# Differential attention: a head's weights are made between the maxima of the next head's two scores

## The chip, the cores and the metric

The kernel runs on one core of a Trainium2 chip. The metric is the device time of one execution in microseconds (us); less is better. Engines are TensorE (PE, its weight loads PEld), VectorE (DVE), ScalarE (ACT), GpSimd (POOL) and SyncE (SP).

## What is computed

Two stacks of two layers each run one after the other over 256 tokens of width 1024. The change lies in the first stack, in its differential attention, which each of its two layers holds once, beside two other kinds of attention and gates. Cut to that branch:

```python
def _diff_branch(q, k, v, lam, subln, lambda_init, cos, sin):
    q = _apply_rope(q.reshape(b, s, DIFF_HEADS, 2, DIFF_D), cos, sin)     # 8 heads, 2 scores each, 64 wide
    k = _apply_rope(k.reshape(b, s, DIFF_HEADS, 2, DIFF_D), cos, sin)
    v = v.reshape(b, s, DIFF_HEADS, 2 * DIFF_D)
    lambda_full = jnp.exp(jnp.sum(lf[0] * lf[1])) - jnp.exp(jnp.sum(lf[2] * lf[3])) + lambda_init
    def attend(qblk):
        sc = jnp.einsum('bqhcd,bkhcd->bhcqk', qblk, k).astype(jnp.float32) * scale
        p = jax.nn.softmax(sc, axis=-1)
        w = (p[:, :, 0] - lambda_full * p[:, :, 1]).astype(v.dtype)
        return jnp.einsum('bhqk,bkhe->bqhe', w, v)
    o = _rms(_sweep_query_blocks(attend, q), subln, 1e-5) * (1.0 - lambda_init)
```

A head has two scores of 256 x 256, two softmaxes, and one matrix of weights, the first softmax less lambda times the second.

## The kernel before

All 256 tokens stay on chip; the projections' weights (about 400 MB) stream in. They come as **panels** of 512 KB (128 x 1024 fp32) through a ring of five buffers `wring`. ACT copies a panel to `whi` (rounded), DVE takes the rest to `wlo` (`split_lo`, 128x1024 TENSOR_TENSOR, L121), and PE multiplies each chunk three times (hi x hi, hi x lo, lo x hi). A panel of a projection is 24 matmuls of 128x256 (L112). ACT's part stands three panels ahead in the order, DVE's two.

`schedule` writes one list of steps. Each engine's program goes through that list and issues its own part of each step, so the list is the order of every engine's queue, and an engine does a later step only when it is through with, or waits no more for, the earlier ones. Two generators are woven: `weave((diff(), 1), (pgate(), 0.75))` takes one turn of the differential attention and then three quarters of a turn of `pgate`, the projections for the gates and one branch product (`xT` and `oM` panels). Each `yield` is such a turn. Of three turns of `pgate` two bring a panel.

Inside `diff`, `staged(8, ...)` runs eight heads through stages. A stage is a function, a lag and a flag:

```python
def staged(n, *stages):
    for i in range(n + max(lag for _, lag, _ in stages)):
        for f, lag, rest in stages:
            if 0 <= i - lag < n:
                f(i - lag)
                if rest or i >= n:
                    yield
```

The stages of head h, with what each issues:

- `scores(0)`, `scores(1)`: PE writes a score of head h to a PSUM bank (L112 `ps<-kT,qT`, four records of 64x256 in the trace for each of the two). DVE takes the row maxima (TENSOR_REDUCE L133, 128x512, and a small TENSOR_SCALAR L124, 128x2): below, a **max**. ACT makes `E` = exp with the sums (two ACTIVATE L118).
- `weights`: `diff_weights` on DVE waits for both exps of the head, then runs two RECIPROCAL (L139), two TENSOR_SCALAR of 128x256 (L124), a small TENSOR_SCALAR with `small`, and two SCALAR_TENSOR_TENSOR of 128x256 (L130).
- `turn_unit`, the **turn**: PE waits for the head's weights and transposes them (four L115 `ps<-cst,E`); DVE copies the result to `PT` (L127, 128x512).
- `values`: PE multiplies `PT` with the values (L112 `ps<-PT,dv`), ACT takes the result to `dsq` (squares) and `draw`.
- `norm`, once in two heads: PE sums the squares, ACT takes the root by Ln and Exp with two table loads. `gain`, once in two heads, on DVE: a product (L130, `draw`), a cast (L127) and a difference (L121) to `oD`.

The score buffers `E` form a ring of four, so two heads are in flight. The branch product's output is taken by DVE to `acc` (L130, 128x512).

Of the kernel before, what the change touches and what calls it, by code (L numbers as in the profile page):

```python
# [330 lines left out]
# [8 lines that stand above are left out]
# [77 lines left out]
def schedule(K, a):  # L416
# [5 lines left out]
    def do(kind, *args):  # L422
        steps.append((kind, args))
# [61 lines left out]
    def turned(src, n, ready, out, w=128):  # L485

        for c in range(0, n, 2):
            m = min(2, n - c)
            u = AB.take()
            do("turn", u, src, c, m, w, ready)  # L490
            out(c, m, u)
            yield
# [16 lines left out]
    def features_to(dst, func=ACT.Copy, scale=1.0, w=128, tag=None):  # L509
        return lambda c, m, u: do("features_out", dst, tag or dst.name, c, m, u, func, scale, w)  # L510
# [11 lines left out]
    def mem_keys(l, x):  # L522
        yield from projB(a["mem_w_kv"][l], 0, 512, x, features_to(memkv[l].mk))

    def mem_values(l, x):
        yield from projA(a["mem_w_kv"][l], 512, 512, x, tokens_to(memkv[l].mv, 512))
# [11 lines left out]
    prow, values = ar.take("prow", 128), mem_values(0, memT)  # L538
# [24 lines left out]
    def rms_open(tag, at, sums, buf=None):  # L563

        n = Box()
        n.tag, n.h = tag, hN.tok()
        n.hold = [buf or ar.take("rms", 2048, at=at), ar.take("rmss", 16, at=sums)]
        n.u3, b = n.hold[0].tok(), n.hold[1].ap
        n.ss, n.pre, n.tmp, n.rs = b[:, 0:4], b[:, 4:6], b[:, 6:8], b[:, 8:10]
        return n  # L570
# [26 lines left out]
    def block1(l, xN, xT, later):  # L597
# [39 lines left out]
        def score_unit(key, q, k, scale, ready):  # L637

            v = Box()
            v.key, v.s = key, ES.take()  # L640
            v.E = v.s.ap[:, 0:512].rearrange("p (t k) -> p t k", t=2)
            v.mx, v.rs = v.s.ap[:, 512:514], v.s.ap[:, 514:516]
            do("scores", v, AB.take(), q, k, scale, ready)
            return v

        def turn_unit(v):

            v.p = PS.take()
            v.PT = v.p.ap.rearrange("p (s q) -> p s q", s=2)
            u = AB.take()  # L650
            do("turn_weights", v, u)
            v.s.freed = u.full
            return v
# [36 lines left out]
        def diff():  # L690
            for k, b in enumerate((dq, dk)):
                do("diff_rope", c, b, kT, k)
                yield
            do("diff_lambda", c, kT)
            c.lam = sm[:, 82:83]
            yield from turned(dq.tok(), 8, lambda h, t: [("diff_rope", l, 0)], features_to(qT, tag=("diff", l, "q")))
            yield from turned(dk.tok(), 8, lambda h, t: [("diff_rope", l, 1)], features_to(kT, tag=("diff", l, "k")))
            ar.give(dq, dk)
            c.oD = None
            un, sqs = {}, {}  # L700
            rings = [[ar.take(k, 512) for _ in range(2)] for k in ("dsq", "draw")]
            SQ, RAW = (Slots(r) for r in rings)

            def scores(i):
                def go(h):
                    un[h, i] = score_unit(("diff", l, h, i), qT.ap[64 * i:64 * i + 64, h * 256:h * 256 + 256],
                                          kT.ap[64 * i:64 * i + 64, h * 256:h * 256 + 256], 0.125, [(("diff", l, x), h) for x in "qk"])
                return go

            def weights(h):  # L710
                do("diff_weights", c, un[h, 0], un[h, 1])
                un[h, 1].s.freed = ("weights", un[h, 0].key, 1)

            def values(h):
                if h % 2 == 0:
                    sqs[h] = (SQ.take(), RAW.take())
                sq, raw = sqs[h // 2 * 2]
                u = AB.take()
                v = un[h, 0]
                do("values", v, dv.tok()[:, :, h * 128:h * 128 + 128], u, lambda: [(dv.name, t, h // 4) for t in range(2)])  # L720
                v.p.freed = u.full
                do("diff_values_out", c, h, u, sq, raw)

            def norm(h):
                if h % 2:
                    do("diff_norm", c, h - 1, AB.take(), sqs[h - 1][0])

            def gain(h):
                if h % 2:
                    sq, raw = sqs[h - 1]  # L730
                    c.oD = c.oD or ar.pair("oD", 8)
                    do("diff_gain", c, h - 1, sq, raw)
                    sq.freed = raw.freed = (c.oD.name, h - 1)
            yield from staged(8, (scores(0), 0, True), (scores(1), 0, True), (lambda h: turn_unit(un[h, 0]), 1, True), (values, 2, True),
                              (norm, 3, False), (weights, 0, False), (gain, 4, False))
            ar.give(qT, kT, dv, *rings[0], *rings[1])

        mqT = ar.take("mqT", 1024)
# [6 lines left out]
        def pgate():  # L745
            yield from projB(w, MQ, 512, xT, features_to(mqT))
            for i in range(2):
                gT.append(gT[0].again() if i else ar.take("gate", 2048, top=True))
                yield from projB(w, GATE + 1024 * i, 1024, xT, lambda k, m, u: do("gate_out", c, i, gT[i], k, m, u))
                if i == 0:  # L750
                    yield from branch(acc, wb, 0, oM, gT[0], 0, keep=True)
                    ar.give(oM)
        weave((diff(), 1), (pgate(), 0.75))
        oD, oE, g2 = c.oD, ar.pair("oE", 4), ar.take("gate", 2048)

# [31 lines left out]
        if l == 0:  # L787
# [5 lines left out]
            keys, values = mem_keys(1, memT), mem_values(1, memT)  # L793
# [76 lines left out]
    norm = rms_open(("mix", 0), None, 34304, n.res.again())  # L870
# [445 lines left out]
    for l in range(DEPTH):  # L1316
        norm = block2(l, norm)
# [1577 lines left out]
```

How the kernel before makes its waits and increments, by code:

```python
    def wait_ge(self, sem, n):  # L106
        if self.e is not None and self.seen.get(id(sem), 0) < n:
            self.e.wait_ge(sem, n)
            self.seen[id(sem)] = n
# [1232 lines left out]
    def bank_free(u):  # L1342
        if u.before:
            e.wait_ge(*at(u.before))
# [1 line left out]
    def tokens(p, x, us, q0, first, fin):  # L1346
        e.wait_ge(*at(("lo", p.i)))
        for t in range(2):
            o = us[t].ap[:, 0:p.nb]
            if first:
                bank_free(us[t])
            for k in range(p.nk):
                e.wait_ge(*at((x.name, q0 + k)))
                xh, xl = x.at(q0 + k, t * 128, 128)
                e.matmul(o, xh, p.hi[:, k, :], start=first and k == 0, stop=False)
                e.matmul(o, xh, p.lo[:, k, :], start=False, stop=False)
                m = e.matmul(o, xl, p.hi[:, k, :], start=False, stop=fin and k == p.nk - 1)
            m.then_inc(*up("pe_panel", ("panel", p.i, t)))
# [1 line left out]
    def features(p, x, u, q0, chunks):  # L1360
        e.wait_ge(*at(("lo", p.i)))
        if q0 == 0:
            bank_free(u)
        for j0 in range(0, p.nb, 128):
            w = min(128, p.nb - j0)
            o = u.ap[0:w, 2 * j0:2 * j0 + 256]
            for k in range(p.nk):
                q = q0 + k
                e.wait_ge(*at((x.name, q)))
                xh, xl = x.at(q)
                ch, cl = p.hi[:, k, j0:j0 + w], p.lo[:, k, j0:j0 + w]
                e.matmul(o, ch, xh, start=q == 0 and j0 == 0, stop=False, skip_group_check=True)
# [292 lines left out]
    def mem_kept():  # L1665
        e.wait_ge(*at("memkept"))
```

## Time and profile before

| | us |
|---|---|
| median of 3 runs | 2539.05 (2537.12 to 2541.59) |
| the profiled execution | 2531.99, span 2530.2 |
| PE busy, share of the span | 2458.0, 97% |
| DVE busy | 1798.4, 71% |
| ACT busy | 1442.6, 57% |
| differential attention's heads, layer 0 | about 174 to 238 us from the span's start |
| the same, layer 1 | about 683 to 747 us |

Starts in the timeline are in us from the span's start. A bracket behind an instruction gives how long its engine stood idle before it, and what released it. Of two consecutive DVE instructions the second's start is the safer mark, since the listed durations overlap a little.

### The profile page before, as it was taken

Reading aid. Unit: us, or ns where it says so; the run is one execution under the profiler, and the core shown is the slowest. Engines: PE = TensorE matmul, PEld = TensorE weight load, DVE = VectorE, ACT = ScalarE, POOL = GpSimd, SP = SyncE. Lnnn points to the kernel's source line nnn. Section 1 sums busy time; section 2 is a strip of 40 time slices with the busy share of each in tenths; the row PEclk is TensorE's granted clock in tenths of the full one; section 3 lists DMA queues with packets and bytes.
Section 4 is the critical chain, followed back from the end, with each engine's and each line's share of the span. In section 5 each row is a group of like instructions: output and inputs, shape, how many; then the busy total and the mean of one; then the engine's idle time right before and its main releaser. Section 6 shows DMA issues by size and latency. Waiting matters only on the chain.

```text
span 2530.2 us, 42246 instructions
## 1 busy us (share of the span) xinstructions
PE 2458.0 (97%) x17296; PEld 2253.4 (89%) x17296; DVE 1798.4 (71%) x2929; ACT 1442.6 (57%) x2106; POOL 268.5 (11%) x222
## 2 busy tenths in 40 slices
PE   8999999999999999899999999999999999999998
PEld 8888989888889898799999798998898999898986
DVE  4567675565676755587778896885697778886874
ACT  5547555445475554466656654664766656545654
POOL 0000002000000000001114710000011207500000
PEclk9999999999999999999999999999999999999999
DMA  7544576655445566554466645666554567545664
GB/s 249 158 129 118 165 241 199 202 181 159 127 119 164 171 196 201 161 152 126 126 196 194 198 131 176 190 205 185 146 151 118 156 190 202 178 152 171 191 201 132
DMA packets 358917, 430.44 MB, mean 170 GB/s; under 512 B 20617, under 2 KB 286311, under 8 KB 358469
## 3 DMA queue, kind: packets, MB, share of 16 engines
q1 hardware_dynamic: 341312, 401.72, 52.3%
q10 hardware_dynamic: 14340, 14.93, 2.4%
q0 software_dynamic: 3072, 11.10, 1.4%
q8 instruction: 137, 2.24, 0.4%
q14 instruction: 56, 0.45, 0.1%
HBM read 424.44 MB, written 3.24 MB: 169 GB/s over the span
## 4 chain that ended last, share of the span: by engine, by line
PE 85%; DVE 8%; ACT 4%; issue 1%; DMA 1%; POOL 0%; POOLq 0%; ACTq 0%; DVEq 0%
PE ps L112 84%; DVE wlo L121 2%; PE ps L115 2%; ACT L118 1%; ACT whi L118 1%; ACT hgKm L118 1%; ACT E L118 0%; ACT lnv L118 0%; DVE hgQB L121 0%; DMA kT<-in_diff_lambda 0%; DVE hgQF L121 0%; DVE E L124 0%; DVE sbc L130 0%; DVE E L133 0%; DVE gate L130 0%
## 5 line engine op out<-in xcount | busy, mean ns | idle before, releaser
L121 DVE TENSOR_TENSOR wlo<-wring,whi 128x1024 fp32r<-128x1024 f32 (+1 forms) x768 | 919.2, 1217 | 264.8 <-ACT whi L118 264.3
L118 ACT ACTIVATE whi<-wring 128x1024 fp32r<-128x1024 f32 (+1 forms) x768 | 801.7, 1053 | 428.7 <-PE ps L112 405.0
L112 PE MATMUL ps<-uT,whi 128*128 128x256 f32 x4640 | 820.9, 281 | 9.5 <-DVE wlo L121 6.3
L112 PEld LDWEIGHTS ps<-uT,whi 128*128 128x128 f32 x4640 | 707.6, 189 | 19.7 <-DVE wlo L121 10.0
L112 PE MATMUL ps<-uT,wlo 128*128 128x256 f32 x2320 | 646.5, 279 | 0.0
L112 PEld LDWEIGHTS ps<-uT,wlo 128*128 128x128 f32 x2320 | 437.8, 189 | 0.0
L112 PE MATMUL ps<-xT,whi 128*128 128x256 f32 x2112 | 376.7, 283 | 2.2 <-DVE xT L121 1.1
L112 PEld LDWEIGHTS ps<-xT,whi 128*128 128x128 f32 x2112 | 321.2, 188 | 10.1 <-issue 6.2
L112 PE MATMUL ps<-xT,wlo 128*128 128x256 f32 x1056 | 294.1, 279 | 0.0
L112 PE MATMUL ps<-whi,hid 128*128 128x512 f32 x864 | 269.4, 391 | 1.6 <-DVE wlo L121 1.6
L112 PEld LDWEIGHTS ps<-xT,wlo 128*128 128x128 f32 x1056 | 198.3, 188 | 0.3
L112 PEld LDWEIGHTS ps<-whi,hid 128*128 128x128 f32 x864 | 162.3, 188 | 36.1 <-DVE wlo L121 2.4
L112 PE MATMUL ps<-wlo,hid 128*128 128x512 f32 x432 | 168.9, 391 | 0.0
L124 POOL TENSOR_SCALAR sE<-mxb,sm 128x256 f32<-128x256 f32 x64 | 106.9, 1679 | 265.6 <-DMA mxb<-spread 253.3
L112 PE MATMUL ps<-whi,xT 128*128 128x512 f32 x384 | 132.3, 406 | 0.0
L112 PE MATMUL ps<-whi,uT 128*128 128x512 f32 x384 | 126.1, 399 | 0.0
L118 ACT ACTIVATE E<-ps,E 128x256 f32<-128x256 f32 x112 | 52.1, 472 | 92.3 <-DVE E L124 92.3
L118 ACT ACT_TABLE_LOAD x79 | 101.4, 1283 | 3.9 <-issue 2.3
L112 PEld LDWEIGHTS ps<-wlo,hid 128*128 128x128 f32 x432 | 81.1, 188 | 17.6
L112 PEld LDWEIGHTS ps<-whi,uT 128*128 128x128 f32 x384 | 72.2, 188 | 17.1 <-DVE wlo L121 1.3
L112 PEld LDWEIGHTS ps<-whi,xT 128*128 128x128 f32 x384 | 72.2, 188 | 16.3 <-issue 1.5
L112 PE MATMUL ps<-whi,merged 128*128 128x512 f32 x256 | 80.9, 392 | 3.3 <-DVE wlo L121 3.3
(394 smaller groups left out, 3577.3 us busy)
## 6 DMA issues: line engine op xcount, KB each, us to landing
wring<-in_w_in SPq DMA_DIRECT2D x346, 512.0 KB, 4.1
wring<-in_mlp_w SPq DMA_DIRECT2D x128, 512.0 KB, 4.3
wring<-in_w_up SPq DMA_DIRECT2D x88, 512.0 KB, 4.6
wring<-in_w_down SPq DMA_DIRECT2D x44, 512.0 KB, 4.6
wring<-in_w_branch SPq DMA_DIRECT2D x32, 512.0 KB, 3.4
wring<-in_w_out SPq DMA_DIRECT2D x32, 512.0 KB, 4.1
wring<-in_mem_w_kv SPq DMA_DIRECT2D x16, 512.0 KB, 6.9
wring<-in_w_br_hg SPq DMA_DIRECT2D x16, 512.0 KB, 5.4
```

What stands on the lines that cost most here:

```text
L112: return self.e.matmul(*p, **k) if self.e else Nothing()
L115: return self.e.transpose(*p, **k) if self.e else Nothing()
L118: return self.e.activation(*p, **k) if self.e else Nothing()
L121: return self.e.tensor_tensor(*p, **k) if self.e else Nothing()
L124: return self.e.tensor_scalar(*p, **k) if self.e else Nothing()
```

## The change

The stage `weights` goes from lag 0, behind `norm`, to lag 1, between `scores(0)` and `scores(1)`:

```diff
-            yield from staged(8, (scores(0), 0, True), (scores(1), 0, True), (lambda h: turn_unit(un[h, 0]), 1, True), (values, 2, True),
-                              (norm, 3, False), (weights, 0, False), (gain, 4, False))
+
+            yield from staged(8, (scores(0), 0, True), (weights, 1, False), (scores(1), 0, True), (lambda h: turn_unit(un[h, 0]), 1, True), (values, 2, True),
+                              (norm, 3, False), (gain, 4, False))
```

So in round i of the loop the order was: scores of head i, turn of head i-1, values of i-2, norm, weights of head i, gain. It is now: first score of head i, weights of head i-1, second score of head i, turn of head i-1, values of i-2, norm, gain. No instruction of the computation is added or taken away.

The first place is DVE's queue in layer 0 around the weights of head 2 (buffers `E_68` and `E_69`). Before:

```order
L121 TENSOR_TENSOR wlo<-wring,whi 128x1024 x2
L139 RECIPROCAL E_68<-E_68 128x2
L139 RECIPROCAL E_69<-E_69 128x2
L124 TENSOR_SCALAR E_68<-E_68 128x256 x2
L124 TENSOR_SCALAR E_69<-E_69,small_59 128x2
L130 SCALAR_TENSOR_TENSOR E_68<-E_69,E_68 128x256 x2
L133 TENSOR_REDUCE E_70<-ps 128x2
L124 TENSOR_SCALAR E_70<-E_70 128x2
L133 TENSOR_REDUCE E_71<-ps 128x2
L124 TENSOR_SCALAR E_71<-E_71 128x2
L127 COPY PT_73<-ps 128x512
```

Now:

```order
L121 TENSOR_TENSOR wlo<-wring,whi 128x1024 x2
L133 TENSOR_REDUCE E_70<-ps 128x2
L124 TENSOR_SCALAR E_70<-E_70 128x2
L139 RECIPROCAL E_68<-E_68 128x2
L139 RECIPROCAL E_69<-E_69 128x2
L124 TENSOR_SCALAR E_68<-E_68 128x256 x2
L124 TENSOR_SCALAR E_69<-E_69,small_59 128x2
L130 SCALAR_TENSOR_TENSOR E_68<-E_69,E_68 128x256 x2
L133 TENSOR_REDUCE E_71<-ps 128x2
L124 TENSOR_SCALAR E_71<-E_71 128x2
L127 COPY PT_73<-ps 128x512
```

The first max of head 3 (`E_70`) went ahead of head 2's weights; nothing else moved. Heads 0, 1 and 3 read alike.

The second place is DVE's queue in layer 0 around the weights of head 5 (`E_70`, `E_71`). Before:

```order
L139 RECIPROCAL E_70<-E_70 128x2
L139 RECIPROCAL E_71<-E_71 128x2
L124 TENSOR_SCALAR E_70<-E_70 128x256 x2
L124 TENSOR_SCALAR E_71<-E_71,small_59 128x2
L130 SCALAR_TENSOR_TENSOR E_70<-E_71,E_70 128x256 x2
L130 SCALAR_TENSOR_TENSOR draw_84<-draw_84,small_59,dsq_82 128x512
L127 CAST oD_89<-draw_84 128x512
L121 TENSOR_TENSOR oD_89<-draw_84,oD_89 128x512
L133 TENSOR_REDUCE E_68<-ps 128x2
L124 TENSOR_SCALAR E_68<-E_68 128x2
L130 SCALAR_TENSOR_TENSOR acc_88<-gate_81,ps 128x512
L133 TENSOR_REDUCE E_69<-ps 128x2
```

Now:

```order
L130 SCALAR_TENSOR_TENSOR draw_84<-draw_84,small_59,dsq_82 128x512
L127 CAST oD_89<-draw_84 128x512
L121 TENSOR_TENSOR oD_89<-draw_84,oD_89 128x512
L133 TENSOR_REDUCE E_68<-ps 128x2
L124 TENSOR_SCALAR E_68<-E_68 128x2
L130 SCALAR_TENSOR_TENSOR acc_88<-gate_81,ps 128x512
L139 RECIPROCAL E_70<-E_70 128x2
L139 RECIPROCAL E_71<-E_71 128x2
L124 TENSOR_SCALAR E_70<-E_70 128x256 x2
L124 TENSOR_SCALAR E_71<-E_71,small_59 128x2
L130 SCALAR_TENSOR_TENSOR E_70<-E_71,E_70 128x256 x2
L133 TENSOR_REDUCE E_69<-ps 128x2
```

The weights went behind the gain's three instructions, the first max of head 6 (`E_68`) and an `acc` step. At heads 4 and 6 the weights went behind the next head's first max and one `wlo`; at head 7 behind the gain alone.

The third place is PE's queue around the turn of head 7 (`cst,E_70`). Before:

```order
L112 MATMUL ps<-xT_52,whi 128x256 x2
L112 MATMUL ps<-xT_52,wlo 128x256
L112 MATMUL ps<-PT_73,dv_79 128x256 x2
L115 MATMUL ps<-cst,E_70 128x128 x4
L112 MATMUL ps<-xT_52,whi 128x256 x2
L112 MATMUL ps<-xT_52,wlo 128x256
```

Now:

```order
L112 MATMUL ps<-xT_52,whi 128x256 x2
L112 MATMUL ps<-xT_52,wlo 128x256
L112 MATMUL ps<-xT_52,whi 128x256 x2
L112 MATMUL ps<-xT_52,wlo 128x256
L115 MATMUL ps<-cst,E_70 128x128 x4
L112 MATMUL ps<-PT_74,dv_79 128x256 x2
L112 MATMUL ps<-xT_52,whi 128x256 x2
L112 MATMUL ps<-xT_52,wlo 128x256
```

In round 8 every stage yields, so the weights of head 7 now bring a turn of `pgate` with them, and one whole panel (24 matmuls) stands between the values of head 5 (`PT_73`) and the turn of head 7. Up to there PE's queue is as it was, and SP's and POOL's queues are as they were everywhere. ACT's queue differs only behind that place, in where two norms stand among `whi` copies. Layer 1 changes in the same way at all places.

## Rows read from the trace of the kernel before

**Rows 1.** The page: the chain that ended last, by engine.
```profile
PE 85%; DVE 8%; ACT 4%; issue 1%; DMA 1%; POOL 0%; POOLq 0%; ACTq 0%; DVEq 0%
```
**Rows 2.** Waits of PE, whole span: us in total, times, longest.
```profile
PE ps L115 <- DVE E L130: 5.5, 4, 2.2
```
**Rows 3.** Timeline, DVE, layer 0: end of weights 2; both maxima of head 3.
```profile
196.77 0.88 DVE L130 SCALAR_TENSOR_TENSOR E<-E,E 128x256 f32<-128x256 f32 x2
198.24 0.69 DVE L133 TENSOR_REDUCE E<-ps 128x2 f32<-128x512 f32 x1 [0.58 <-PE ps L112]
...
199.04 0.68 DVE L133 TENSOR_REDUCE E<-ps 128x2 f32<-128x512 f32 x1
```
**Rows 4.** Timeline, PE, layer 0: scores of head 3, turn 2, next panel.
```profile
197.07 1.14 PE L112 MATMUL ps<-kT,qT 64*128 64x256 f32 x8
198.14 0.66 PE L115 MATMUL ps<-cst,E 128*128 128x128 f32 x4
198.56 0.48 PE L112 MATMUL ps<-xT,whi 128*128 128x256 f32 x2
```
**Rows 5.** Timeline, DVE, layer 0: start of weights 0.
```profile
181.36 0.23 DVE L139 RECIPROCAL E<-E 128x2 f32<-128x2 f32 x2 [1.14 <-ACT E L118]
```
**Rows 6.** Timeline, layer 0, head 1: its weights' start, its turn, next panel.
```profile
188.19 0.22 DVE L139 RECIPROCAL E<-E 128x2 f32<-128x2 f32 x2
...
189.86 0.85 PE L115 MATMUL ps<-cst,E 128*128 128x128 f32 x4 [2.07 <-DVE E L130]
...
190.47 0.48 PE L112 MATMUL ps<-xT,whi 128*128 128x256 f32 x2
```
**Rows 7.** Timeline, DVE, layer 0: first max of head 5, the wlo behind.
```profile
212.38 0.69 DVE L133 TENSOR_REDUCE E<-ps 128x2 f32<-128x512 f32 x1 [0.25 <-PE ps L112]
...
213.18 1.22 DVE L121 TENSOR_TENSOR wlo<-wring,whi 128x1024 fp32r<-128x1024 f32 x1
```
**Rows 8.** Timeline, PE, layer 0: turn 4.
```profile
216.35 0.66 PE L115 MATMUL ps<-cst,E 128*128 128x128 f32 x4
```
**Rows 9.** Timeline, DVE, layer 0: weights 5, gain, first max 6, acc, second max 6.
```profile
219.60 0.22 DVE L139 RECIPROCAL E<-E 128x2 f32<-128x2 f32 x2
...
221.44 0.74 DVE L130 SCALAR_TENSOR_TENSOR draw<-draw,small,dsq 128x512 f32<-128x512 f32 x1
...
223.30 0.68 DVE L133 TENSOR_REDUCE E<-ps 128x2 f32<-128x512 f32 x1
...
224.10 0.69 DVE L130 SCALAR_TENSOR_TENSOR acc<-gate,ps 128x512 f32<-128x512 f32 x1
224.70 0.68 DVE L133 TENSOR_REDUCE E<-ps 128x2 f32<-128x512 f32 x1
```
**Rows 10.** Timeline, PE, layer 0: scores of head 6; panel behind turn 5.
```profile
220.54 1.14 PE L112 MATMUL ps<-kT,qT 64*128 64x256 f32 x8
...
222.02 0.48 PE L112 MATMUL ps<-oM,whi 128*128 128x256 f32 x2
```
**Rows 11.** Timeline, PE, layer 0: first score of head 7, turn 6.
```profile
226.70 1.13 PE L112 MATMUL ps<-kT,qT 64*128 64x256 f32 x4
...
231.75 0.66 PE L115 MATMUL ps<-cst,E 128*128 128x128 f32 x4
```
**Rows 12.** Timeline, layer 0, head 7: its weights' start and its turn.
```profile
235.12 0.22 DVE L139 RECIPROCAL E<-E 128x2 f32<-128x2 f32 x2
...
236.79 0.85 PE L115 MATMUL ps<-cst,E 128*128 128x128 f32 x4 [0.70 <-DVE E L130]
```
**Rows 13.** Timeline, PE, layer 0: values 1, behind the panel that began at 198.56.
```profile
201.39 1.02 PE L112 MATMUL ps<-PT,dv 128*128 128x256 f32 x4
```
**Rows 14.** Stretches: us, PE, PEld, DVE, ACT, POOL busy, granted clock, DMA share, GB/s.
```profile
186.00:191.00 5.00, 2.93 (x23) 2.20 (x22) 4.47 (x13) 2.01 (x4) 0.00 (x0) 1.00 0.63 201
1040.00:1050.00 10.00, 3.40 (x16) 2.95 (x16) 7.85 (x16) 3.60 (x9) 3.09 (x3) 0.66 0.00 0
1200.00:1240.00 40.00, 37.45 (x311) 37.28 (x311) 39.77 (x64) 23.11 (x34) 8.70 (x7) 0.96 0.45 120
```

## The prediction

> **What bounds the kernel now.** I read the chain that ended last first. It runs through PE for 85% of the span [rows 1], so what PE loses is lost to the kernel unless a later wait of PE gives it back, and what DVE or ACT lose counts only where PE waits for them. Then PE's waits: for a head's weights on DVE it waited 5.5 us in four places [rows 2], which are the turns of heads 1 and 7 in both layers. Last I read the timeline of DVE and PE side by side at each head. The reader is to see there how much room lies between the end of a head's weights on DVE and PE's arrival at that head's turn. At head 2 the weights end at 197.65 (196.77 and 0.88) [rows 3] and PE comes to the turn at 198.14 [rows 4]: 0.49 us of room. PE's two scores of head 3 stand directly ahead of that turn, with no panel between, and DVE is then idle: the first max of head 3 waits 0.58 us for its score. The weights of head 2 are thus made while PE still works at a panel.
>
> **The change, part by part.** No work is added. What counts is that the weights of head h now stand behind the first max of head h+1 on DVE, and so behind PE's score for it, and that PE's turn of head h waits for those weights.
>
> Three durations do the whole sum. From the start of a pair of scores to the start of the first max it is 198.24 - 197.07 = 1.17 us. A max takes 199.04 - 198.24 = 0.80 us of DVE [rows 3, 4]. From the start of the weights to PE's first matmul behind a turn that waited for them it is 190.47 - 188.19 = 2.28 us, and to the start of the turn 189.86 - 188.19 = 1.67 us [rows 6].
>
> Heads 2 and 3: now PE's next panel can begin 1.17 + 0.80 + 2.28 = 4.25 us after the scores' start. Before it began 198.56 - 197.07 = 1.49 us after it [rows 4]. That is +2.76 us each. Head 3 has the same order on both engines, and layer 1 repeats layer 0, so there are four of them: +11.04 us. The bounds: without the max's own 0.80 it would be 1.96 us each, and 0.80 more, if a second max came between, 3.56. I take 2.76, since each of its parts is from these very instructions. Nothing covers this: PE's queue is in order, and the only matmuls ahead of the turn are the scores.
>
> Head 5: its weights go behind the gain, the first max of head 6 and an `acc` step. The gain takes 223.30 - 221.44 = 1.86 us [rows 9]. It would run from 219.60 to 221.46, still before the score arrives at 220.54 + 1.17 = 221.71 [rows 10], so it is hidden under that wait. The `acc` step takes 224.70 - 224.10 = 0.60 us and is not hidden; its panel ended at 220.54, so it has nothing to wait for. The next panel begins 1.17 + 0.80 + 0.60 + 2.28 = 4.85 us after the scores, before 222.02 - 220.54 = 1.48 [rows 9, 10]. That is +3.37 us, twice: +6.74 us.
>
> Head 1: here PE waited before. It reached the turn at 189.86 - 2.07 = 187.79 [rows 6]. At head 2 the first score had arrived 0.10 us after PE reached the turn (198.24 and 198.14) [rows 3, 4], so here the first max can start at about 187.89, the weights at 188.69 and the next panel at 190.97 in place of 190.47: +0.5 us. This needs DVE to be free 0.3 us earlier than it was, when the weights began at 188.19. It should be: the first max of head 1 now runs in the 1.14 us in which DVE waited for head 0's exps [rows 5], which leaves head 0's weights where they are, and brings head 1's second max, ACT's exp and the `whi` and `wlo` behind it forward by up to 0.80 us. The bounds are 0 and 0.80; I take 0.5, twice: +1.0 us. Head 0 itself costs nothing, by that same idle time, with 0 and 0.80 as bounds.
>
> Heads 4 and 6: a panel stands between the next head's first score and the turn, and it is the cover. At head 4 the first max still starts at 212.38 and the `wlo` at 213.18 [rows 7]; with 1.22 us for it the weights begin by 214.40, and the turn could start 1.67 us later, at 216.07. PE arrives at 216.35 [rows 8]. At head 6 the first max starts at 226.70 + 1.17 = 227.87, the weights begin at 227.87 + 0.80 + 1.22 = 229.89, and the turn could start at 231.56; PE arrives at 231.75 [rows 11]. Both cost nothing, with 0.3 and 0.2 us of room, and each microsecond more on DVE would be paid in full. What is late next there is the last of the four transposes, by 0.1 us at most.
>
> Head 7: the weights go behind the gain, 235.12 + 1.86 = 236.98, and work behind the turn could begin at 236.98 + 2.28 = 239.26 [rows 9, 12]. PE reached this turn at 236.79 - 0.70 = 236.09 [rows 12], and now runs one panel first, 201.39 - 198.56 = 2.83 us [rows 4, 13], to 238.92, and a turn without a wait takes 198.56 - 198.14 = 0.42: 239.34. Before, turn and panel together ended at 236.79 + 0.61 + 2.83 = 240.23. That is -0.9 us, twice: -1.8 us. The old wait of head 7 goes.
>
> Behind DVE's new wait stand the second max, the `PT` copy and the `wlo` of later panels. They come later by DVE's clock but not by PE's, which stands still for the same time, and a `wlo` has two panels (5.7 us) of lead; I cost them at nothing. DMA gains time, as its transfers wait for freed buffers only. The score buffers are released in the same order.
>
> What the gaps do to PE's clock is the one cost with no row of its own. PE now stands still 199.04 + 1.67 - 198.14 = 2.57 us at heads 2 and 3, 2.6 at head 1 and 3.2 at head 5. With its wait of 2.07 us at head 1 it was granted 1.00, that is 2.4 GHz; about a gap of 8 us the mean fell to 0.66, with 1.2 GHz in part of it [rows 14]. The new gaps are much nearer to the first, so I take nothing; the other end is in the rivals. The Trainium skill's page "TensorE: Matmul & The Clock Gate", section "Why this matters for your kernels", speaks against this change: idle gaps between bursts of matmuls should be avoided, since one of them can bring the engine back to the lower clock. The trace shows that for the long gap and not for the 2.07 us one. By the rows the sum is +17.0 us; by that rule, at the cheap price below, it would be +26.6.
>
> **Sum.** 11.04 + 6.74 + 1.0 - 1.8 = +17.0 us. Against the profiled execution's own 2531.99 that makes 2549.0. The median of the runs shown lies 7.1 us above that execution, and it is the median that a new measurement answers to, so I add the sum to 2539.05: **2556 us**, 0.67% slower. A measurement of this kernel can tell about 0.2%, 5 us, from no change.
>
> **The rivals.**
> - *Forecast, 74%*: six turns exposed, clock kept: 2556 us.
> - *The clock falls in the gaps, 10%.* For it: the new gaps are longer than the 2.07 us one. Against it: they are far from 8 us. The smallest fall in the trace, a mean of 0.96 over 40 us, is worth 1.6 us of PE's full clock, the one of 0.66 over 10 us 3.4 [rows 14]. At six gaps that is +9.6 to +20 us more: 2566 to 2576; the cheap end is the likelier.
> - *Half of it is given back, 9%*: DVE, ACT and DMA gain a lead while PE stands still, and PE's later waits for `wlo` shrink. Against it: those waits come behind work that itself hangs on PE. +8.5 us: 2547.5.
> - *Covered after all, 5%*: the weights would still be ready in time, or the new places would not act. Only heads 1 and 7 change: +1.0 - 1.8, 2538 us. It would need about 2.6 us between the first score and the turn of heads 2, 3 and 5, where PE's queue has 1.07.
> - *Faster, 2%*: the earlier maxima bring ACT's exps forward, DVE works ahead, and PE's old waits of 5.5 us all go [rows 2]: 2533.5 us. It decides at the same point, whether DVE has the first max done 1.67 us before PE reaches the turn; at the heads that cost here it has not even got the score.
>
> **How the numbers follow.** The range 2547 to 2566 takes in the half given back and the clock's cheap end, and the bounds of the terms (about 5 us down, 4 up). It leaves out the last two cases and the clock's dear end, and something for what I don't see. Slower is the first three cases, 93%; within 0.2% is the fourth, 5%; faster the fifth, 2%.
>
> **What would show it.** In the new profile PE waits at L115 for DVE's L130 in eight places and about 21.7 us: four of 2.6 at heads 2 and 3, two of 2.6 at head 1, two of 3.2 at head 5. In the timeline each first max waits for PE's score with the weights right behind it. At heads 0, 4, 6 and 7 no wait is longer than 0.3 us. The granted clock around 180 to 250 us stays at 1.00. I am wrong if the turns wait and the span doesn't grow by that sum (then PE gets it back later), if heads 4 and 6 wait too (then the room was misread), or if the clock falls.

## The result, and the profile after

The changed kernel took 2558.65 us in the median of 6 runs (2553.90 to 2565.82), the kernel before 2538.16 in 6 (2536.46 to 2541.59). The ratio is 1.0083, 95% interval 1.0068 to 1.0097: slower by 0.83%, about 21 us. The profiled execution of the changed kernel took 2563.81 us, span 2562.0, near the upper end of them.

The page of the changed kernel, busy time, and the chain that ended last by engine (before: [rows 1]; PE was busy 2458.0 us):

```profile
PE 2473.4 (97%) x17296; PEld 2268.9 (89%) x17296; DVE 1800.0 (70%) x2929; ACT 1443.9 (56%) x2106; POOL 269.1 (11%) x222
...
PE 82%; DVE 11%; ACT 3%; issue 2%; POOL 1%; DMA 1%; ACTq 0%; POOLq 0%; DVEq 0%
```

DVE's share of the chain rose from 8% to 11% with hardly any more work on DVE. And PE was busy 15 us longer with the same 17296 matmuls, which the moved waits alone can't do.

Waits of PE in the changed kernel over the whole span: us in total, times, longest.

```profile
PE ps L115 <- DVE E L130: 21.3, 8, 3.1
PE ps L112 <- DVE wlo L121: 13.7, 17, 1.8
```

Against [rows 2] the waits at the turns rose from 5.5 us in four places to 21.3 in eight. The other waits stayed: for `wlo` 13.7 us in 17 places, before 12.7 in 16.

Timeline of the changed kernel, layer 0, around the turn of head 2: first PE's scores of head 3, the turn and the panel behind it, then DVE (start, us, what, idle before). These answer to [rows 3, 4].

```profile
196.02 1.14 PE L112 MATMUL ps<-kT,qT 64*128 64x256 f32 x8
199.67 0.85 PE L115 MATMUL ps<-cst,E 128*128 128x128 f32 x4 [2.51 <-DVE E L130]
200.28 0.48 PE L112 MATMUL ps<-xT,whi 128*128 128x256 f32 x2
...
197.18 0.69 DVE L133 TENSOR_REDUCE E<-ps 128x2 f32<-128x512 f32 x1 [5.38 <-PE ps L112]
...
197.99 0.23 DVE L139 RECIPROCAL E<-E 128x2 f32<-128x2 f32 x2
...
199.84 0.68 DVE L133 TENSOR_REDUCE E<-ps 128x2 f32<-128x512 f32 x1
```

DVE stands idle for 5.38 us with the weights of head 2 behind the max that waits for PE; the score comes 1.16 us after the scores began, the weights start 0.81 later, and PE's next panel 2.29 after that. From the scores to the panel it is 4.26 us, where before it was 1.49.

The same at head 5, first PE from its scores of head 6 on, then DVE ([rows 9, 10] before):

```profile
226.72 1.14 PE L112 MATMUL ps<-kT,qT 64*128 64x256 f32 x8
230.97 0.85 PE L115 MATMUL ps<-cst,E 128*128 128x128 f32 x4 [3.12 <-DVE E L130]
231.58 0.62 PE L112 MATMUL ps<-oM,whi 128*128 128x256 f32 x2
232.00 0.42 PE L112 MATMUL ps<-oM,wlo 128*128 128x256 f32 x1
...
227.88 0.69 DVE L133 TENSOR_REDUCE E<-ps 128x2 f32<-128x512 f32 x1 [0.17 <-PE ps L112]
...
228.69 0.69 DVE L130 SCALAR_TENSOR_TENSOR acc<-gate,ps 128x512 f32<-128x512 f32 x1
229.29 0.22 DVE L139 RECIPROCAL E<-E 128x2 f32<-128x2 f32 x2
```

The max and the `acc` step stand ahead of the weights, the gain is hidden ahead of the max: from the scores to the panel it is 231.58 - 226.72 = 4.86 us, before 1.48. And the panel behind the turn is slow: a `wlo` matmul takes 0.42 us here where one takes 0.28 elsewhere.

The granted clock says why. Stretches of the changed kernel over the two stages (us, then busy time of PE, PEld, DVE, ACT, POOL, granted clock, DMA share, GB/s), and the same two of the kernel before:

```profile
170.00:240.00 70.00, 59.34 (x393) 51.71 (x392) 43.95 (x97) 37.88 (x94) 0.00 (x0) 0.93 0.34 98
690.00:770.00 80.00, 69.33 (x469) 61.04 (x468) 52.73 (x116) 45.86 (x111) 0.00 (x0) 0.94 0.35 98
```
```profile
170.00:240.00 70.00, 67.22 (x495) 59.09 (x494) 55.79 (x122) 47.74 (x115) 0.00 (x0) 1.00 0.43 122
690.00:770.00 80.00, 77.23 (x572) 68.92 (x572) 62.95 (x131) 58.15 (x129) 0.00 (x0) 1.00 0.42 119
```

Turn by turn it is not the same everywhere. The 4 or 5 us behind the turns of heads 2 and 3 in layer 0:

```profile
199.70:204.70 5.00, 5.00 (x28) 4.81 (x29) 3.94 (x6) 2.12 (x6) 0.00 (x0) 0.66 0.21 40
212.20:216.20 4.00, 4.00 (x31) 3.75 (x32) 3.11 (x6) 2.10 (x6) 0.00 (x0) 1.00 0.09 11
```

Over the 5 us from the turn's start the mean is 0.66 or 0.67 behind six of the eight waits, and 1.00 behind that of head 3 in both layers. In part of each stage, then, PE ran at 1.2 GHz in place of 2.4. That is worth 0.07 x 70 + 0.06 x 80 = 9.7 us of PE's full clock, an estimate; a single fall is worth 0.34 x 5 = 1.7 us. So this execution's 31.8 us over the profiled one of before are made up roughly like this: the turns about 17, the clock in the stages about 10, and the rest, about 5, outside. There the changed kernel ran by an order that is not changed at all, but the clock fell for longer at two places where it falls in both kernels (mean 0.81 from 1070 to 1100 us where before it was 0.91 from 1044 to 1074; 0.87 from 1806 to 1846 where before it was 0.96 from 1780 to 1820). That part is spread between runs: of the changed kernel's six runs the fastest, 2553.90 us, had a mean clock of 0.990, and the two slowest, 2563.81 and 2565.82 us, had 0.986 and 0.987.

Two marks give the cost by layer. From the first score of layer 0 (174.08 us before, 171.26 after) to that of layer 1 (682.92 and 693.35) the changed kernel took 13.3 us more; from there to the transposes of the first stack's last norm (857.13 and 880.62) 13.1 more. Both layers lose the same, and nothing is given back before the stack ends.

### The profile page after: what moved, and what is told of

Same layout as the page of the kernel before. It is cut to its first block, busy times and chain, and to the rows that moved or that the text cites. A ratio compares the mean times of both kernels' runs of the same rounds, so it can differ in the third digit from the quotient of the medians.

```text
span 2562.0 us, 42246 instructions
## 1 busy us (share of the span) xinstructions
PE 2473.4 (97%) x17296; PEld 2268.9 (89%) x17296; DVE 1800.0 (70%) x2929; ACT 1443.9 (56%) x2106; POOL 269.1 (11%) x222
## 4 chain that ended last, share of the span: by engine, by line
PE 82%; DVE 11%; ACT 3%; issue 2%; POOL 1%; DMA 1%; ACTq 0%; POOLq 0%; DVEq 0%
PE ps L112 80%; DVE wlo L121 3%; PE ps L115 2%; POOL sE L124 1%; DVE sE L121 1%; ACT L118 1%; ACT hgKm L118 1%; DMA mxb<-spread 0%; ACT whi L118 0%; DVE sE L124 0%; ACT lnv L118 0%; DVE hgQB L121 0%; DMA kT<-in_diff_lambda 0%; DVE ys L130 0%; DVE hgQF L121 0%
## 5 line engine op out<-in xcount | busy, mean ns | idle before, releaser
L112 PE MATMUL ps<-xT,whi 128*128 128x256 f32 x2112 | 383.4, 285 | 2.5 <-DVE xT L121 1.3
L133 DVE TENSOR_REDUCE E<-ps 128x2 f32<-128x512 f32 x56 | 38.6, 689 | 72.0 <-PE ps L112 71.6
L112 PEld LDWEIGHTS ps<-whi,xT 128*128 128x128 f32 x384 | 72.2, 188 | 16.2 <-issue 1.5
```

The costliest lines, as they stand in the source:

```text
L112: return self.e.matmul(*p, **k) if self.e else Nothing()
L133: return self.e.tensor_reduce(*p, **k) if self.e else Nothing()
```

## The experiments

Each ratio is to the kernel before, measured beside it on the same chip. There it took 2531.4 us (first four experiments), 2534.8 (next three) and 2533.8 (last two), so the ratios are what to compare. Of each edit only the part of the line that differs is shown.

### The changed kernel again

No edit.

> The changed kernel once more, unaltered, to see how far it spreads from run to run and whether its granted clock falls at the same turns. Theory (eight waits at the turns, 17 us, and on top of them falls of PE's clock that differ from run to run): profile again with eight waits of DVE's L130 at L115, 21 to 22 us; runs between 2553 and 2566 us, a lower mean clock going with a longer time, about 1 us for each 0.0004 of clock. Rival (the waits alone cost about 21 us and the clock's falls in the first profile were an accident of that run): runs within 3 us of each other, clock as in the kernel before.

2556.72 us (2553.14 to 2563.24, 5 runs), ratio 1.0100 (1.0085 to 1.0114). Again eight waits of 21.3 us, and mean clocks of 0.986 to 0.990 against 0.987 to 0.993 of the kernel before. Two runs with 0.986 took 2560.69 and 2563.24 us, the one with 0.990 took 2553.14, but a third with 0.986 took 2556.72: the clock accounts for most of the spread and not for all. The clock did not fall at the same turns. These are the turns of head 1 in layer 1, first here, then in the first profile of the changed kernel:

```profile
713.96 0.85 PE L115 MATMUL ps<-cst,E 128*128 128x128 f32 x4 [2.51 <-DVE E L130]
```
```profile
709.58 1.21 PE L115 MATMUL ps<-cst,E 128*128 128x128 f32 x4 [2.51 <-DVE E L130]
```

The wait is the same to 0.01 us. The mean clock in the 5 us behind it was 1.00 here and 0.66 there; over this profile it fell behind five of the eight waits. Behind this one the same four transposes took 0.85 us at the higher clock and 1.21 at the lower.

### PE kept busy in its waits

The needless transposes add PE work that the reference has not; the turn overwrites what they write.

```diff
         p3 = u.ap.rearrange("p (s q) -> p s q", s=2)
+        if v.key[0] == "diff":
+            for _ in range({1: 16, 2: 16, 3: 16, 5: 20}.get(v.key[2], 0)):
+                e.transpose(p3[:, 0, 0:128], ident, ident)
         for s in range(2):
```

> The changed kernel, with 16 (heads 1 to 3) or 20 (head 5) needless transposes of a constant that PE runs ahead of the turns that wait, about 2.2 and 2.8 us, into the bank that the turn then overwrites. The waits for the weights stay, only PE is not idle in them. Theory (waits 17 us, the rest is the clock): no fall of the clock around the turns, next panel 2.3 us behind the weights' start as before, time 17 us over the kernel before, 2553 to 2556 us, with a spread of a few us, so 3 to 8 us less than the changed kernel. Rival (the clock costs nothing that shows): the same time as the changed kernel or more.

2548.57 us, ratio 1.0064 (1.0049 to 1.0079), where the unaltered changed kernel has 1.0100. Timeline of PE at head 1 (scores, the 16 transposes, the turn), and the stretches over both stages:

```profile
185.79 1.14 PE L112 MATMUL ps<-kT,qT 64*128 64x256 f32 x8
186.86 1.97 PE L115 MATMUL ps<-cst 128*128 128x128 f32 x16
189.35 0.94 PE L115 MATMUL ps<-cst,E 128*128 128x128 f32 x4 [0.52 <-DVE E L130]
```
```profile
170.00:240.00 70.00, 67.46 (x498) 58.82 (x496) 47.84 (x106) 42.59 (x104) 0.00 (x0) 1.00 0.36 105
690.00:770.00 80.00, 77.46 (x574) 68.38 (x573) 56.91 (x123) 48.95 (x116) 0.00 (x0) 1.00 0.36 107
```

The panel behind the turn comes no earlier: 4.26 us behind the scores here (185.79 to 190.05) and 4.86 at head 5, as in the changed kernel. Yet the clock stays at 1.00 and 0.36% of the time comes back, 9 us of about 25. The mean clocks say the same, as an estimate: 0.992 in the median of these runs, 0.986 in the unaltered changed kernel's, 0.991 in the kernel before's. What is left, 0.64% or 16.2 us, is the waiting by itself: the sum of the prediction was 17.0. From the first score of layer 1 (692.08) to the last norm (874.59) it is 182.5 us, 8.3 more than before; half of the sum is 8.5.

### The turn behind a panel, in the changed order

```diff
-(scores(0), 0, True), (weights, 1, False), (scores(1), 0, True), (lambda h: turn_unit(un[h, 0]), 1, True), (values, 2, True),
+(scores(0), 0, True), (weights, 1, False), (scores(1), 0, True), (values, 2, True), (lambda h: turn_unit(un[h, 0]), 1, True),
```

> The changed order, with the turn behind the values of the head before, so that a panel of 2.8 us and the values of 0.7 us stand between the second score and the turn at heads 1, 2, 3 and 5. DVE's order of maxima and weights is the changed one (the PT copy moves with the turn). Theory (the loss is that PE has nothing between the score and the turn): room of 3.5 us against waits of 2.5 to 3.1, so no wait over 0.3 us is left at these turns, and the old ones of heads 1 and 7 go too: about 2533 us (2530 to 2538). Rival (the late weights themselves cost, by the wlo and exps behind them): 2545 us or more, with waits of PE for wlo in the stage.

2526.18 us (11 runs), ratio 0.9984 (0.9972 to 0.9996): faster than the kernel before by about 4 us. Waits of PE, and the timeline at head 1: first DVE (first max of head 2, weights of head 1), then PE from the scores of head 2 to the turn of head 1, with a panel left out between:

```profile
PE ps L115 <- DVE E L130: 1.1, 2, 0.6
```
```profile
186.11 0.69 DVE L133 TENSOR_REDUCE E<-ps 128x2 f32<-128x512 f32 x1 [0.46 <-PE ps L112]
...
186.91 0.23 DVE L139 RECIPROCAL E<-E 128x2 f32<-128x2 f32 x2
...
184.94 1.14 PE L112 MATMUL ps<-kT,qT 64*128 64x256 f32 x8
186.01 1.13 PE L112 MATMUL ps<-PT,dv 128*128 128x256 f32 x4
...
189.81 0.60 PE L115 MATMUL ps<-cst,E 128*128 128x128 f32 x4
```

DVE still has the weights behind the first max: at head 1 the max waited for its score until 186.11 and the weights started at 186.91. But PE now comes to the turn at 189.81, with a panel done meanwhile, and doesn't wait. The two waits left are at head 7, 0.56 us in each layer, behind the gain. So late weights cost nothing as such; what cost was that nothing stood between the score and the turn.

### The turn behind a panel, in the order before

```diff
-(scores(0), 0, True), (scores(1), 0, True), (lambda h: turn_unit(un[h, 0]), 1, True), (values, 2, True),
+(scores(0), 0, True), (scores(1), 0, True), (values, 2, True), (lambda h: turn_unit(un[h, 0]), 1, True),
```

> The kernel before, with the turn behind the values of the head before. Theory: its 2.1 us waits at head 1 go, since a panel now covers them; in round 8 the values of head 6 follow its turn with only PT's copy between, which may cost 1 us in each layer: 2533 to 2537 us. Rival (nothing to gain, since those waits are made up elsewhere): 2538 us.

2526.71 us (11 runs), ratio 0.9975 (0.9965 to 0.9984). The waits for weights are gone and two short ones for PT's copy have come, as expected:

```profile
PE ps L112 <- DVE PT L127: 1.7, 2, 0.9
```

The gain is larger than expected: 2533 to 2537 us were set against a kernel before of about 2538, 1 to 5 us under it, and it is 6.3. The waits account for 5.5 - 1.7 = 3.8 us of it. The mean clock was 0.993 in the median of these runs and 0.991 in the kernel before's, but how much of the rest goes with that was not tested.

### The weights ahead of both maxima

```diff
-(scores(0), 0, True), (weights, 1, False), (scores(1), 0, True),
+(weights, 1, False), (scores(0), 0, True), (scores(1), 0, True),
```

> The weights at lag 1 as in the change, but ahead of both scores of the next head instead of between them. PE's order is that of the changed kernel. Theory (the loss is that the weights wait behind a max that waits for PE's score): nearly all of the loss goes; at head 5 the gain's 1.9 us still stand ahead of the weights, so a wait of about 1.8 us at its turn in both layers, head 1 keeps its 2.1, head 7 loses its 0.7: +3.6 - 1.8, about 2540 us (2537 to 2543). Rival (lag 1 itself, the extra yield or the gain ahead of the weights, is what costs): 2550 us or more.

2536.06 us (10 runs), ratio 1.0001 (0.9988 to 1.0013). The loss is gone with the max that stood ahead of the weights, and lag 1 with its extra yield costs nothing. Timeline, turns of heads 1 and 5 in layer 0:

```profile
187.45 1.21 PE L115 MATMUL ps<-cst,E 128*128 128x128 f32 x4 [2.07 <-DVE E L130]
...
222.15 0.85 PE L115 MATMUL ps<-cst,E 128*128 128x128 f32 x4 [1.45 <-DVE E L130]
```

Head 5 waits 1.45 us behind the gain, 0.4 less than expected. Head 1 is as in [rows 6], with the same 2.07 us, but there the clock stayed up and here the transposes took 1.21 us and the mean clock of the 5 us from the turn's start was 0.66: it fell at this very wait. In layer 1 of this same execution head 1 waited 2.07 us too, and the clock stayed at 1.00.

### The weights behind both maxima

```diff
-(scores(0), 0, True), (weights, 1, False), (scores(1), 0, True),
+(scores(0), 0, True), (scores(1), 0, True), (weights, 1, False),
```

> The weights at lag 1 behind both maxima of the next head: a second max of 0.80 us stands ahead of them too. PE's order is that of the changed kernel. Theory: at heads 1, 2, 3 and 5 the turn waits 0.8 us longer than in the changed kernel, 3.3, 3.3, 3.3 and 3.9, and at heads 4 and 6, where the second score stands directly ahead of the turn, waits of about 2.5 to 3.3 us appear that the changed kernel has not: in both layers together 8 x 0.8 = 6.4 and 4 x 2.8 = 11.2 more, so 35 us over the kernel before without the clock, 2573 us, and with its falls 2575 to 2590. Rival (it is the length of DVE's queue and not the place of the score that counts): heads 4 and 6 stay without a wait and the time is about 6 us over the changed kernel, 2565.

2586.56 us (4 runs), ratio 1.0216 (1.0185 to 1.0246), about 55 us over the kernel before. The expected 2575 to 2590 were set against a kernel before of 2538, 37 to 52 us over it, so this is a little above the range. Waits of PE, and the turns of heads 0, 1 and 4 in layer 0:

```profile
PE ps L115 <- DVE E L130: 40.7, 14, 3.9
```
```profile
183.10 0.85 PE L115 MATMUL ps<-cst,E 128*128 128x128 f32 x4 [1.45 <-DVE E L130]
191.16 1.21 PE L115 MATMUL ps<-cst,E 128*128 128x128 f32 x4 [3.31 <-DVE E L130]
...
231.78 1.21 PE L115 MATMUL ps<-cst,E 128*128 128x128 f32 x4 [2.53 <-DVE E L130]
```

Head 1 waits 0.80 us longer than in the changed kernel, the price of the second max, and head 4, which had no wait there, waits 2.53: now its second score stands directly ahead of its turn. The rival, which had heads 4 and 6 stay without a wait, is out. Missed was head 0, with 1.45 us in both layers: a `wlo` of 1.13 us stands ahead of its weights too. The waits grew by 40.7 - 5.5 = 35.2 us over the kernel before. The other 20 fit the clock, 0.981 to 0.985 in these runs against 0.989 to 0.993 in the kernel before's: 0.0075 of the span is 19 us, an estimate from the mean clocks. In the profile it fell behind all twelve waits of 2.5 us or more, and behind neither of 1.45.

### The change in layer 1 only

```diff
+            if l == 1:
+                yield from staged(8, (scores(0), 0, True), (weights, 1, False), (scores(1), 0, True), ...
+            else:
+                yield from staged(8, (scores(0), 0, True), (scores(1), 0, True), ...
```

> The change in layer 1 only; layer 0 keeps the order before. Theory (the cost is made in each layer by itself and never given back): half, about 8.5 us of waits and 1 to 4 us by the clock, 2547 to 2551 us, four long waits in layer 1 and the old ones in layer 0. Rival (the two layers' stages share a cost, or a later stage gives a part back): clearly off half, under 2544 or over 2554.

2548.11 us (4 runs), ratio 1.0049 (1.0033 to 1.0065), 12.4 us: about half of what the whole change cost in its two measurements, 1.0083 and 1.0100. Six waits, 13.3 us, as 10.7 of the change and 2.7 of the old ones. Layer 0 has the order of the kernel before here, and yet at head 1 the clock fell behind the old wait, with a mean of 0.67 over the 5 us from the turn's start:

```profile
188.51 1.21 PE L115 MATMUL ps<-cst,E 128*128 128x128 f32 x4 [2.06 <-DVE E L130]
```

So the kernel before can lose clock at that turn as well; that its own profile has 1.00 there [rows 14] was one execution.

### Both moves together, and the late turn again

The weights stand at lag 1 ahead of both scores, and the turn behind the values:

```diff
+(weights, 1, False), (scores(0), 0, True), (scores(1), 0, True), (values, 2, True), (lambda h: turn_unit(un[h, 0]), 1, True),
+(norm, 3, False), (gain, 4, False)
```

> The weights at lag 1 ahead of both scores, and the turn behind the values of the head before. Theory (a turn waits only where fewer microseconds of PE's work than of DVE's stand between the last release of its weights and itself): a panel covers heads 1, 2, 3 and 5, the weights are ready at heads 4 and 6, and in the last rounds a panel stands behind the turn of head 6, so no wait for L130 over 0.3 us and none for PT's copy is left: 2 to 3 us under the changed order with the late turn in waits, about 5.5 us under the kernel before, ratio about 0.998. Rival (what is left of the waits is nothing against the spread, or a gain ahead of the weights makes a new one): no better than the late turn alone, ratio 0.9975 or above.

> The kernel before with the turn behind the values of the head before, once more beside the last candidate on the same chip. Theory: 5.5 us of waits gone, 1.7 us of new ones at PT's copy, so 3.8 us by the waits and one or two by the clock: ratio 0.9975 to 0.9985 again. Rival: the first result was spread, ratio 1.000.

2529.15 us (12 runs), ratio 0.9978 (0.9963 to 0.9993), and beside it the late turn in the order before: 2529.51 us (12 runs), 0.9982 (0.9968 to 0.9996). The waits for weights of the first are 1.1 us in two places, not none: at head 7 the gain still stands ahead of the weights, and PE waits 0.56 us there. So the rival holds that had it no better than the late turn alone. The two can't be told apart. That the late turn is faster than the kernel before by about 0.2% is shown in all four measurements, each with an interval below 1; which version with it is the best stays open.

## Why the prediction was right, and where it was not

The forecast was 2556 us, the measured median 2558.65; the way, the size and the waits were right. That the clock keeps was wrong, and that the number came out so near is in part luck. By its steps:

**Heads 2 and 3**, +2.76 us each: measured 4.26 us from the scores to the panel against the predicted 4.25. Right to 0.02 us, in all four places with a wait of 2.51 to 2.52 (predicted 2.57).

**Head 5**, +3.37: wait of 3.12 us in both layers, predicted 3.17; from the scores at 226.72 to the panel at 231.58 it is 4.86 us against 4.85. The gain was hidden under the wait for the score, as said.

**Head 1**, +0.5 us: its wait rose from 2.07 to 2.51, +0.44 (in layer 1 from 2.15 to 2.51, +0.36). The step that the earlier max brings ACT's exp and the `whi` behind it forward held: the max of head 2 already waited for its score (0.46 us idle in the first profile), so DVE was there in time.

**Heads 0, 4 and 6**, nothing: no wait. **Head 7**, -0.9: no wait in either layer. From the start of head 6's turn to the values of head 6, with the same work between, it was 8.56 us (231.75 to 240.31) and is 7.36 (242.97 to 250.33), so -1.2 us; in layer 1 -1.0. The step took PE's arrival from the idle time, 236.09; but PE's next matmul can begin 0.68 us behind the start of the values (246.29 and 246.97 in the new profile), which is 235.75, and the panel thus ends about 0.3 us sooner. The eight waits sum to 21.3 us; the prediction said 21.7.

**The sum.** 17.0 us was the predicted price of the order. The terms as measured at full clock, 11.1 for heads 2 and 3, 6.8 for head 5, 0.8 for head 1 and -2.2 for head 7, make 16.5, and the run with PE kept busy measured it at 16.2 us (12.4 to 20.0 by its interval). The tests of the mechanism agree: taking away the max ahead of the weights takes the loss away, a second max adds 0.80 us at each such turn and makes heads 4 and 6 wait, and a panel between score and turn takes all of it away though DVE's order stays.

**The step that failed** is "so I take nothing" for what the gaps do to PE's clock. It rested on one row: with its wait of 2.07 us at head 1 PE was granted 1.00 [rows 14]. That row was an instance, not a rule. With the weights ahead of both maxima the clock fell at that same wait of 2.07 us, and with the change in layer 1 only it fell in layer 0, in the very order of before. Of the eight waits in the first profile of the changed kernel it fell behind six, and in its second profile behind five. So the forecast's case, turns exposed and clock kept, is not what happened; the rival of the clock, given 10%, is, and at about its cheap end: it asked for +9.6 us, and it was 9.7 us in the two stages of the profiled execution, 9 us by the difference of the ratios 1.0100 and 1.0064. It reached that with 1.6 us at six gaps, though the prediction itself lists eight waits of 2.6 us and more; that six of eight fell is luck.

The result came out near 2556 nonetheless since its ratio in the first measurement, 1.0083, took in 4 us over the sum. In the second, at 1.0100, it was 8 us. The page "TensorE: Matmul & The Clock Gate" of the Trainium skill, section "Why this matters for your kernels", warns that an idle gap between bursts of matmuls can bring the clock down. The trace agrees that it can, behind six of the eight waits. The page says it of gaps longer than the waits of 2.51 us at heads 1 to 3, so the prediction's +26.6 us, with a fall at six gaps, was more than it states; the second measurement, 25.3 us, is nearer to that sum than to 17.0.

**The other rivals.** Nothing was given back: waits for `wlo` did not shrink, and both layers' shifts, 13.3 and 13.1 us, were still there at the stack's end. Covered after all, and faster: no; each needed work between the score and the turn, and where the late turn put it there, both came true.

**What stays open** is when the clock falls behind a wait of 2 to 3 us. The same wait at the same turn did and did not, in two executions of one kernel, and no run here controls it. The length of the wait goes with it, by the granted clock in the 5 us from each turn's start. At the turns of the differential attention it fell behind 27 of 32 waits of 2.51 to 3.92 us (the changed kernel twice, the change in layer 1 only, and the weights behind both maxima), behind 2 of 5 of 2.06 to 2.15 us, and behind none of 19 of 1.45 us or less, eight of them behind the needless transposes.

## What to carry to other kernels

Before an instruction is moved on one engine, look at what it will stand behind, and what that waits for: 0.80 us of max cost 2.76 because it put PE's next work behind an answer of DVE to PE's own score. Count the work of the waiting engine between the last thing it hands over and the thing it waits for; if that is more than the other engine's way back, the order on the other engine is free, and if not, move the waiting step and not the work. And price a new gap on PE twice, once for the wait and once for the clock behind it, even if a shorter gap in the trace went by without.

## What the runs showed of the hardware

A wait of 2.07 us on PE was followed by the higher clock in one layer and by 1.2 GHz in part of the next 5 us in the other, in one execution of one kernel (the weights ahead of both maxima). Waits of 2.51 us were followed by either in two executions of the changed kernel. No wait of 1.45 us or less at these turns, 19 in all, was followed by the lower clock, and all twelve of 2.5 to 3.9 us in the profile with the weights behind both maxima were. At the lower clock four transposes took 1.21 us in place of 0.85 when it held for all of them, and a 128x256 matmul 0.41 to 0.42 us in place of 0.28. A fall with a mean of 0.66 over 5 us, as behind most of these turns, cost 1.7 us of PE's full clock, an estimate.

PE work without any use, 16 transposes of a constant in 1.97 us at each of three turns and 20 at a fourth in both layers, kept the clock at 1.00 in both stages, and the changed kernel's ratio went from 1.0100 to 1.0064.
